# Router scores inside the output projection, tokens turned once, bias terms and expert 0's weights brought in early: one core, two hybrid blocks and a mixture of experts

## What is computed

```python
for l in range(DEPTH_2):
    h = rmsnorm(x, norm1_g[l])
    x = x + hybrid_mixer(h, w_in[l], ..., w_out[l])
    h = rmsnorm(x, norm2_g[l])
    x = x + moe_ffn(h, w_router[l], b_router[l], w_gate[l], b_gate[l], ...)
return rmsnorm(x, normf_g)

def moe_ffn(h, ...):
    logits = xt @ w_router + b_router
    top_vals, top_idx = lax.top_k(logits, TOP_K)      # 4 of 32 experts
    top_gates = jax.nn.softmax(top_vals, axis=-1)
    ...                                               # tokens sorted by expert, in blocks
    gate = jnp.minimum(xb @ w_gate[e] + b_gate[e], SWIGLU_LIMIT)
    up = jnp.clip(xb @ w_up[e] + b_up[e], -SWIGLU_LIMIT, SWIGLU_LIMIT)
    y = (gate * sigmoid(1.702 * gate) * (up + 1.0)) @ w_down[e] + b_down[e]
```

## Time and profile before

| | us |
|---|---|
| median of 3 runs | 3359.95 (3353.88 to 3361.49) |
| the profiled execution | 3351.33, of which the span is 3349.6 |
| mixer | 1640 to 1988 |
| routing | 1988 to 2078 |
| experts | 2078 to 3307 |
| last gather, sums and norm | 3307 to 3349 |

### The profile page before, as it was taken

The page is one execution under the profiler, slowest core; times in us unless marked ns, Lnnn a source line. Parts: engine busy times, 40 slices in busy tenths (PEclk is TensorE's granted clock), DMA queues, the critical chain, the costliest instruction groups (busy, mean ns, idle before and its releaser), DMA issues.

```text
span 3349.6 us, 36990 instructions
## 1 busy us (share of the span) xinstructions
PE 2969.8 (89%) x13196; PEld 1796.7 (54%) x13196; DVE 1369.1 (41%) x2205; ACT 776.4 (23%) x1092; POOL 123.7 (4%) x160
## 2 busy tenths in 40 slices
PE   8799989999799989999787666899998999999884
PEld 8577668888577667888576345233332333333221
DVE  7673646564473547565365644111111111111113
ACT  0563432222363333222232111010110000000001
POOL 0000000000000000000200012000000000000001
PEclk6899999999899999999898786999999999999997
DMA  9323026563323012243422004958489989989995
GB/s 332 115 76 88 14 88 181 160 184 91 105 85 89 1 51 83 75 113 91 138 96 64 0 18 178 409 210 330 149 319 410 410 322 385 410 312 409 410 410 212
DMA packets 392567, 638.38 MB, mean 191 GB/s; under 512 B 28198, under 2 KB 278182, under 8 KB 392458
## 3 DMA queue, kind: packets, MB, share of 16 engines
q1 hardware_dynamic: 375354, 593.44, 49.5%
q0 software_dynamic: 8944, 30.15, 2.5%
q10 hardware_dynamic: 8160, 13.38, 1.2%
HBM read 610.96 MB, written 25.95 MB: 190 GB/s over the span
## 4 chain that ended last, share of the span: by engine, by line
PE 70%; DVE 9%; DMA 7%; SPq 6%; ACT 5%; issue 3%; POOL 0%; ACTq 0%; DVEq 0%; another core or an unknown queue 0%
PE bank L2037 22%; PE bank L132 12%; PE bank L134 12%; PE bank L133 12%; SPq L1932 5%; DMA ring<-w_down 3%; DMA ring<-w_gate 2%; PE bank L939 2%; PE bank L773 1%; PE bank L2042 1%; PE bank L774 1%; DMA RAW<-w_in 1%; PE bank L2029 1%; PE bank L692 1%; PE bank L814 1%
## 5 line engine op out<-in xcount | busy, mean ns | idle before, releaser
L2037 PE MATMUL bank<-ring,xT 128*64 128x512 f32 x3200 | 718.6, 595 | 47.1 <-DMA ring<-w_gate 23.3
L132 PE MATMUL bank<-HH,WHI 128*128 128x512 f32 x1360 | 549.0, 404 | 77.5 <-DVE HL L474 45.2
L133 PE MATMUL bank<-HL,WHI 128*128 128x512 f32 x1360 | 534.0, 393 | 0.0
L134 PE MATMUL bank<-HH,WLO 128*128 128x512 f32 x1360 | 533.8, 393 | 0.0
L2037 PEld LDWEIGHTS bank<-ring,xT 128*64 128x64 f32 x3200 | 219.7, 137 | 495.7 <-issue 382.4
L2037 PE MATMUL bank<-ring,hT 128*64 128x512 f32 x1600 | 360.9, 595 | 30.0 <-DMA ring<-w_down 28.3
L132 PEld LDWEIGHTS bank<-HH,WHI 128*128 128x128 f32 x1360 | 258.6, 190 | 151.5 <-issue 52.1
L457 DVE TENSOR_TENSOR WLO<-RAW,WHI 128x2048 fp32r<-128x2048 f32 (+1 forms) x118 | 248.4, 2107 | 134.8 <-ACT WHI L250 134.8
L2002 DVE TENSOR_SCALAR gc<-bank 128x512 f32<-128x512 f32 x50 | 34.6, 692 | 640.9 <-PE bank L2037 631.0
L133 PEld LDWEIGHTS bank<-HL,WHI 128*128 128x128 f32 x1360 | 259.1, 191 | 53.2 <-issue 3.4
L134 PEld LDWEIGHTS bank<-HH,WLO 128*128 128x128 f32 x1360 | 258.1, 190 | 54.7
(11 more groups left out here) (395 smaller groups left out, 3224.6 us busy)
## 6 DMA issues: line engine op xcount, KB each, us to landing
ring<-w_gate SPq DMA_DIRECT2D x128, 1024.0 KB, 11.6
ring<-w_up SPq DMA_DIRECT2D x128, 1024.0 KB, 13.1
ring<-w_down SPq DMA_DIRECT2D x128, 1024.0 KB, 17.4
RAW<-w_ffn_in SPq DMA_DIRECT2D x88, 512.0 KB, 5.2
RAW<-w_in SPq DMA_DIRECT2D x37, 1024.0 KB, 5.9
ada<-w_ada SPq DMA_DIRECT2D x24, 1024.0 KB, 12.0
RAW<-w_ada SPq DMA_DIRECT2D x24, 1024.0 KB, 5.2
RAW<-w_ffn_out SPq DMA_DIRECT2D x32, 704.0 KB, 4.8
```

The source lines that it names most:

```text
L132: pe.matmul(out, lhi, rhi, start=start, stop=False)
L133: pe.matmul(out, lhi, rlo, start=False, stop=False)
L134: return pe.matmul(out, llo, rhi, start=False, stop=stop)
L2037: ins = pe.matmul(out[halves(h), :], xT[:, k % 4, halves(k // 4)], m["ring"][:, c, at:at + 512], start=False, stop=k == KD - 1)
```

## The change

Six edits:

1. **Scores in the output projection.** After the second, third and fourth out chunk PE takes in two finished tiles of X each (`scored`), and the last two at the end: per tile and 128 tokens one matmul of 128x32 on the raw X with the router's weights, and one of 128x1 on its square, for the sum of squares per token. The router's weights get the norm's gain beforehand on DVE. The root and its reciprocal are now 128x4, and the scores are scaled by it when they are read.
2. **Tokens turned once.** PE turns only X; ACT copies it twice from the bank, once scaled by the reciprocal root (h2t). ACT's queue issues the stores. The gain is applied when a block's tokens are put in xT: by DVE now, with a tile n2x, in every block and in block 0.
3. **Bias terms in the mixer.** POOL splits the bias rows as 128x768 tiles and stores them to memory; SP loads bp in one piece. The zeros are stored after that. DVE waits for the terms before the u step.
4. **Expert 0 preloaded.** SP loads all 12 chunks of expert 0 when the last out group is done (the last chunk when the scores are), and block 0 counts as fresh only if its expert isn't 0.
5. **The one-hot tiles**: ohb in one instruction of 128x1056, ohp in 16 buffers, without the waits for PE.
6. The meeting of all engines after the mixer is gone.

```diff
@@ phases_of
+            mix_program(eng, who, mix, m, b, W)
             if who == "pool":
                 zero_results(eng, MIN_BLOCKS + 1, MAXB - MIN_BLOCKS)
                 eng.wait_ge(zeroed, (MAXB - MIN_BLOCKS) * 16)
-            else:
-                mix_program(eng, who, mix, m, b, W)
-            phase_end(eng, after_mix)
...
@@ mix_program, sp, before the load of chunk ("o", 0)
                 sp.dma_start(m["pw"][:], ...)
+                sp.dma_start(m["wr"][:], W["w_router_2"][0].rearrange("(k p) e -> p k e", p=P))...
+                sp.dma_start(m["brow"][:], W["b_router_2"].broadcast_to([P, EXPERTS]))...
@@ mix_program, pool (new)
+        for i, name in enumerate(("b_gate_2", "b_up_2", "b_down_2")):
+            pool.dma_start(m["bf"][:, i, :], W[name][0].rearrange("e (q n) -> (e q) n", q=4))...
+        pool.wait_ge(*sg.event("bias"))
+        pool.wait_ge(*sg.event("hl", KD - 1))
+        for j in range(3):
+            pool.tensor_copy(m["bt"][:, j], m["bf"][:])...
+            for i in range(3):
+                pool.dma_start(W["terms"][i, 32 * j:32 * j + 32, :].rearrange(...), m["bt"][:, j, i, :])...
+            if j < 2:
+                pool.tensor_tensor(m["bf"][:], m["bf"][:], m["bt"][:, j], ALU.subtract)...
+        pool.wait_ge(*sg.event("terms"))
@@ mix_program, act, out stage
+        def square(k):
+            act.wait_ge(*sg.event("x2", k))
+            if k >= 2:
+                act.wait_ge(*sg.event("rsq_used", k - 2))
+            act.activation(m["sq"][:, k % 2, :], X[:, k, :], ACT.Square)...
@@ mix_program, dve, behind feed(MIX_AT["out", 2]) and ahead of the heads
+        v.wait_ge(*sg.event("router"))
+        for k in range(KD):
+            ins = v.tensor_scalar(m["wr"][:, k, :], m["wr"][:, k, :], vec[:, V2_N2 + k:V2_N2 + k + 1], None, ALU.mult)
@@ mix_program, pe
+        def scored(k):
+            pe.wait_ge(*sg.event("x2", k))
+            for t in range(NT):
+                pe.matmul(b[4 + t][:, 0:EXPERTS], X[:, k, t * P:(t + 1) * P], m["wr"][:, k, :], start=(k == 0), ...)
+            pe.wait_ge(*sg.event("rsq", k))
+            for t in range(NT):
+                ins = pe.matmul(b[4 + t][:, EXPERTS:EXPERTS + 1], m["sq"][:, k % 2, t * P:(t + 1) * P], one[:, 0:1], ...)
...
+            if kind == "out" and i:
+                scored(2 * i - 2)
+                scored(2 * i - 1)
...
+        scored(KD - 2)
+        scored(KD - 1)
@@ route_program, sp
+        sp.wait_ge(*mix.event("acc", MIX_FIRST["out", 3] + 1))
...
+        sp.dma_start(m["bp"][:].rearrange("r (w n) -> r w n", w=3), W["terms"].rearrange("w r n -> r w n"))...
+        for c in range(MOE_SLOTS):
+            if c == MOE_SLOTS - 1:
+                sp.wait_ge(*mix.event("logits"))
+            moe_load(sp, m, W, c, 0).then_inc(mo.sem["mo_first"], 16)
+        sp.wait_ge(mo.sem["mo_first"], 16 * MOE_SLOTS)
         sp.wait_ge(*sg.event("bei"))
@@ route_program, act
+        for t in range(NT):
+            ins = act.activation(m["rs4"][:, t:t + 1], b[4 + t][:, EXPERTS:EXPERTS + 1], ACT.Sqrt, ...)
+        act.wait_ge(*sg.event("rstd"))
+        for g in range(8):
+            t, half = g // 2, slice((g % 2) * 512, (g % 2 + 1) * 512)
+            act.wait_ge(*sg.event("tg", g))
+            act.activation(m["x2t"][:, t, half], b[g % 4][:], ACT.Copy)
+            act.activation(m["h2t"][:, t, half], b[g % 4][:], ACT.Identity, scale=m["rs4"][:, t:t + 1])...
+            if g % 2:
+                act.wait_ge(*sg.event("evac", g))
+                act.dma_start(W["h2tok"][t * P:(t + 1) * P, :], m["h2t"][:, t, :])...
@@ route_program, dve
-            v.scalar_tensor_tensor(m["h2T"][:, k, :], X[:, k, :], vec[:, V2_N2 + k:V2_N2 + k + 1], m["rstdm"][:], ...)
...
+            ins = v.scalar_tensor_tensor(L[:, 32 * t:32 * t + 32], b[4 + t][:, 0:EXPERTS], m["rs4"][:, t:t + 1], m["brow"][:], ALU.mult, ALU.add)
...
+        v.tensor_tensor(m["ohb"][:], ...broadcast_to([P, 16, NB + 1]), ...broadcast_to([P, 16, NB + 1]), ALU.is_equal)...
         for n in range(16):
+            v.tensor_scalar(m["ohp"][:, n, :], m["i64"][:], m["pk"][:, n:n + 1], vec[:, V2_TOK + t:V2_TOK + t + 1], ...)
+...
+        for k in range(KD):
+            v.tensor_scalar(m["n2x"][:, k % 4, k // 4 * BLK:(k // 4 + 1) * BLK], one[:, 0:BLK], vec[:, V2_N2 + k:V2_N2 + k + 1], None, ALU.mult)
...
         v.wait_ge(*sg.event("tx0"))
         v.memset(m["hh"][:], 0.0)
+        v.tensor_tensor(m["xT"][:], b[7][:].rearrange("p (k n) -> p k n", k=NT), m["n2x"][:], ALU.mult)
@@ moe_act, moe_dve
-        act.wait_ge(*sg.event("u", loop=i))
-        act.activation(m["xT"][:], b[7][:], ACT.Copy)...
         v.tensor_scalar(uc, b[1][:], SWIGLU_LIMIT, -SWIGLU_LIMIT, ALU.min, ALU.max)...
+
+        v.tensor_tensor(m["xT"][:], b[7][:].rearrange("p (k n) -> p k n", k=NT), m["n2x"][:], ALU.mult)...
```

More of the change, by code:

```diff
@@ L1096, in _ @@
             mix_program(sp, "sp", mix, m, b, W)
-            gather(sp)
-            route_program(sp, "sp", route, m, b, W, moe)
+            route_program(sp, "sp", route, m, b, W, moe, mix)
             moe_sp(sp, moe, m, W, blocks(sp, "sp"))
@@ L1413, in mix_program @@
                 if i == 0:
+                    v.wait_ge(*sg.event("terms"))
                     v.memset(m["upad"][:, :, 0:16], 0.0)
@@ L1714, in route_program @@
+        act.wait_ge(*sg.event("nmx"))
+        for t in range(NT):
+            ins = act.activation(m["gates"][:, 4 * t:4 * t + 4], m["mxm"][:, 8 * t:8 * t + 4], ACT.Exp,
+                                 bias=m["nmx"][:, t:t + 1], accum_out=m["gs"][:, t:t + 1])
+        ins.then_inc(*sg.inc("ro_act", "gexp", also=[("gexp", None)]))
         act.drain().then_inc(mo.sem["mo_act"], mo.total("mo_act"))
```

192 lines of the change are left out of this document (80 added, 112 removed).

## The result

The changed kernel takes 3306.78 us (median of 4, 3302.57 to 3311.68), the one before, timed beside it, 3356.91 us (median of 4, 3353.63 to 3361.49): ratio 0.9848, 95% interval 0.9834 to 0.9861, 50.1 us less. The forecast was 3304, with 55.5 us less.

What follows compares the result with a forecast made beforehand. PE was taken to bound most of the span, with small-step chains in the routing and full DMA engines in the first expert blocks. Terms summed to -55.5 us, taking the median 3359.95 to 3304.5, given as 3304; range 3284 to 3323.

Steps and rivals of the forecast that it cites:

- Start of the mixer: First weights in the mixer no longer share DMA with the stores of zeros, so squares' second round starts sooner: 12.4 us gained.
- Bias terms and zeros: POOL's bias splitting and later zeros in the mixer cost nothing, 7 us to spare; 5 us if PE's cover is gone.
- Router loads and gain: Router's loads ahead of chunk o,0 lose 1.6 us; its gain on DVE ahead of the first decay loses 1.2.
- Scores: Out stage: 128 score passes at 0.111 us cost 14.2 us; scores still stand 35.5 us sooner, that cost already taken off.
- rival C: PE's clock falls: score passes take 0.222 us, ranks slow too; +14.2 + 3.5 us, 3322 us; chance 8%.
- Scores to tokens: Routing, from scores to tokcol's end: a shorter one-hot tail gains 1.3 us, bounds 0 and 4.
- Tokens to block 0: From tokcol's end to block 0: the gather keeps its time, xT behind the memset on DVE loses 0.7 us.
- Experts: First expert blocks: preloaded down weights leave the full load stream, 10.5 us gained; xT on DVE before gate 1 loses 0.7.
- A: The mixer's start gives nothing, as bias loads, another late step or the postponed zeros replace the wait: 3316.9 us; chance 14%.
- B: The preload does nothing and the first expert blocks stay as long as they are: 3315 us; chance 12%.
- E: Slower: in the out stage a score pass costs as much as a 128x512 one, 64.9 us more, 3369 us; chance 1.5%.
- D: More than forecast: first blocks give 17 us, clock kept in mixer's second round and one-hot tail: 3293.7 us; chance 13%.

## Why the prediction came out as it did

Right in its main parts, and too high in their sum: by 5 us against the medians (55.5 for 50.1) and by 7 against the two profiled spans (48.7), which the parts below add up to. One small part came out right by luck.

- **Start of the mixer**, forecast 12.4. The squares' second round began at 1655.00, as worked out (1655.3). 11.35 arrived at nh: PE's second round took 10.4 us where it took 9.5. The clock had fallen in the gap ahead of it both times, and came back 6 us into the round instead of 4. The cause was put to the test and holds (+7.5 us in time with the zeros back, 7.9 of the stretch).
- **Bias terms and zeros**, forecast nothing. Right, and on the condition that was named. The room was smaller than the 7 us that I gave: the last zeros landed at 1734.1, 1.5 us ahead of SP's next load. 31 of the 32 went out in the 26 us that I took; the last one was issued 9 us behind them. DVE lost some 2.5 us in the gate rows, covered by PE; with the cover gone the same work costs 8.2 us, more than the 5 that I gave.
- **Router loads and gain**, forecast 1.6 and 1.2: 1.45 and 1.17. The first is right by luck. The loads did cost 1.9 us at the first o chunk, near what I gave; but PE then waits less ahead of the u products and keeps its clock, so that 0.5 us is left at the first yp, and another 0.95 comes at a pooling product that now runs at half clock (2.07 us for 1.12). Moving the loads away gave only 0.3 back.
- **The heads**, not in the sum: 1.6 lost. The step that failed is the price of the gain, taken as the 1.2 us of its own instructions: PE waits behind it at the first decay step, its clock falls there, and the runs show 1.7 us more for it (the first dn at 15.5 us behind dec instead of 13.9).
- **Scores**, forecast 14.2 at 0.111 us a pass. Passes took that in the pairs (3.6 us for 32), and the mis-sized term is the clock: 10.55 in the loop instead of 7.1, and 8.4 us instead of 7.1 behind it (1990.66 to the roots at 1999.10), with the last tile at half clock. The 0.2 us for the reciprocal had no row behind it; it took 0.18. My rival C had the clock fall for the passes themselves; it fell behind them, and the wide products paid, about 5 us in all against C's 17.7. C's second half, the ranks at half clock, came only where the scores were edited: 1.9 us with spread scores, 2.9 with wide squares, under its 3.5.
- **Scores to tokens**, forecast 1.3: L began at 2000.06 and its end to tokcol's end is 28.7 us against 30.3, 1.6 gained. The one-hot tail ran at 0.22 us a pass, as taken.
- **Tokens to block 0**, forecast 0.7 lost: level, 0.1 gained. From PE's turn to T0 it is 2.47 us, 2.52 before: xT's 0.63 fell into a gap that was there between the memset and PE's start. The gather took 6.2 us to PE's turn, as long as before, but 1.6 to 1.8 longer than with the DMA engines empty. I had looked only at whether the stores of h2t would be late, not at the preload's end beside the gather.
- **Experts**, forecast 10.5 less 0.7: 8.9, with 9.8 shown for the four chunks alone. The difference is block 0's gate, at a low clock for longer: 9.7 us, 8.6 before (7.0 in later blocks).
- **The rivals.** A, B and E are excluded by the runs, D did not come. What of C came is above.

## What to carry to other kernels

When work moves onto an engine that is already full, read the granted clock in windows of 2 us right behind each group of it: here 3.6 us of one-column and 32-column products made the wide ones behind them pay 1.6 us more in two of three cases, and spreading them, or making half of them wide, took that away. Then look at the next small stage: the ranks lost 2 to 3 us to the clock once the scores no longer did. A few short steps ahead of a product that PE waits for can cost more than themselves (here 1.2 us, and 1.7 more by the clock). When a path is shortened, look at which transfer now ends beside its new end: a preload that was free held the gather and the next load as soon as the path ahead of them was 3 us shorter. And if two edits each give nothing, see by stretches whether each is hiding the other's gain.

## What the runs showed of the hardware

- PE's granted clock fell to half while PE was busy without a break, right behind 3.6 us of f32 products with 32 and with 1 moving columns, in 11 of 16 cases in eight traces. It did not behind 1.8 us of the same (18 cases in three traces), nor behind 3.6 us in which the one-column products were made 128 wide (both cases in one trace).
- At the first decay step a wait of PE of 2.8 to 3.0 us went with a fall of its clock right behind it, and 1.7 us lost, in nine traces of nine; where the wait was 1.6 us it did not fall there, in four of four.
- An f32 product 128x128 by 128x1 and one by 128x128 took nearly the same: eight passes in 0.9 and 0.97 us, start to start, at full clock.
- A DVE step of 0.42 us on four partitions took 2.39 us beside a POOL subtraction of 128x768. The same subtraction made an HL step of 0.69 us take 2.30.
- The gather of 64 rows, from tokcol's end to PE's first turn: 4.4 to 4.7 us with the DMA engines empty, 4.7 to 7.4 with loads of a megabyte each still in flight, the longer the later they landed.
- The broadcast load of the router's bias (one row of 32 to 128 partitions) occupied SP's queue for 1.67 us behind the loads of pw and wr in the kernel after, for 2.90 us behind two chunks and wr in the run with the router moved, and for 0.44 us in the kernel before, at the start of the routing: the time is not the load's own.
